# A two-layer block on one core: the experts' tail and the second projection as one program, worked token tile by token tile

## The reference

```
y = y + combine[:, e:e + 1] * (h @ w_down[e])      # 32 experts, 2 of them per token
h = h + y
x = rmsnorm(h, final_norm_g)                       # result of the first block
h = rms_norm(x, norm_gain)                         # start of the second block
proj = h @ w_in                                    # 1024 x 8448
qa, ka, va, qb, kb, vb, ga, gb, mg = split(proj)
```

## Time and profile before

| | us |
|---|---|
| median of three runs (range) | 1345.03 (1338.94 to 1348.52) |
| profiled execution: time / span of its instructions | 1341.23 / 1339.5 |
| loop of experts, first to last product | 485.1 to 708.3 |
| rows of experts loaded back, sums and norms on DVE | 716.7 to 740.2 |
| PE without an instruction | 719.4 to 741.9 |
| first product of the second projection | 747.8 |
| its units 0, 1, 2 end | 766.9, 778.4, 789.9 |

### The profile page before, as it was taken

How to read it: one execution, slowest core, us unless ns; L and a number is a source line. 1 busy time by engine, 2 the same in 40 slices (tenths; PEclk the granted TensorE clock), 3 DMA queues, 4 the chain that set the end, 5 groups by cost and what they waited for, 6 DMA issues and landing times. The chain is left out here.

```text
span 1339.5 us, 24510 instructions
## 1 busy us (share of the span) xinstructions
PE 1233.6 (92%) x10443; PEld 967.9 (72%) x10443; DVE 549.3 (41%) x973; ACT 491.6 (37%) x859; POOL 153.8 (11%) x210
## 2 busy tenths in 40 slices
PE   5999999999979769999881899999999999999988
PEld 5787775699959545655540798888896678888888
DVE  3433563344364223333225423344437764553242
ACT  4324537603244401111112424455547654332230
POOL 4000003200000001111100001122210015300000
PEclk9999999999999969999996899999999999999999
DMA  4332100000029699999995445422217118222031
GB/s 158 115 104 72 32 1 0 10 4 4 4 70 390 231 367 418 419 418 420 417 409 198 119 139 132 104 92 71 91 32 95 65 36 282 63 64 94 1 110 48
DMA packets 92664, 197.63 MB, mean 148 GB/s; under 512 B 9687, under 2 KB 73261, under 8 KB 79629
## 3 DMA queue, kind: packets, MB, share of 16 engines
q1 hardware_dynamic: 87228, 185.57, 39.6%
q0 software_dynamic: 4752, 8.40, 1.7%
q10 hardware_dynamic: 576, 2.10, 0.4%
HBM read 186.05 MB, written 17.86 MB: 152 GB/s over the span
## 5 line engine op out<-in xcount | busy, mean ns | idle before, releaser
L650 DVE TENSOR_TENSOR w_in_low<-w_in_raw,w_in_high 128x2048 fp32r<-128x2048 f32 x20 | 45.9, 2293 | 116.4 <-ACT w_in_high L642 116.4
L1935 PE MATMUL hidden_ps<-w_gate,gathered_t 128*64 128x256 f32 x384 | 92.2, 395 | 0.3 <-DVE gathered_t L2030 0.3
L1935 PE MATMUL hidden_ps<-w_up,gathered_t 128*64 128x256 f32 x384 | 92.2, 395 | 0.0
L602 PE MATMUL proj_ps<-block_in_high,w_in_low 128*128 128x512 f32 x232 | 90.5, 390 | 0.0
L602 PE MATMUL proj_ps<-block_in_low,w_in_high 128*128 128x512 f32 x232 | 90.5, 390 | 0.0
L602 PE MATMUL proj_ps<-block_in_high,w_in_high 128*128 128x512 f32 x232 | 90.4, 390 | 0.0
L1476 PE MATMUL wo_ps<-w_out_high,wo_x_high 128*128 128x256 f32 x256 | 74.2, 290 | 3.5 <-DVE w_out_low L661 3.5
L2775 PE MATMUL gate_ps<-block_in_high,gate_w_high 128*128 128x512 f32 x192 | 76.0, 396 | 1.0 <-PEq L2444 1.0
L2775 PE MATMUL gate_ps<-block_in_low,gate_w_high 128*128 128x512 f32 x192 | 74.9, 390 | 0.0
L2775 PE MATMUL gate_ps<-block_in_high,gate_w_low 128*128 128x512 f32 x192 | 74.8, 390 | 0.0
L1476 PE MATMUL wo_ps<-w_out_high,wo_x_low 128*128 128x256 f32 x256 | 73.2, 286 | 0.0
(11 more groups left out here) (474 smaller groups left out, 3072.5 us busy)
## 6 DMA issues: line engine op xcount, KB each, us to landing
w_down<-exp_w_down_dram SPq DMA_DIRECT2D x27, 1024.0 KB, 27.9
w_gate<-exp_w_gate_dram SPq DMA_DIRECT2D x24, 1024.0 KB, 20.2
w_up<-exp_w_up_dram SPq DMA_DIRECT2D x24, 1024.0 KB, 23.1
w_in_raw<-w_in_dram SPq DMA_DIRECT2D x20, 1024.0 KB, 5.6
slot_scratch_and_keys<-w_in_dram SPq DMA_DIRECT2D x14, 1024.0 KB, 5.4
vb<-w_in_dram SPq DMA_DIRECT2D x6, 1024.0 KB, 5.8
gate_w_raw_odd<-w_in_dram SPq DMA_DIRECT2D x6, 1024.0 KB, 6.1
slot_scratch_and_keys<-exp_w_down_dram SPq DMA_DIRECT2D x5, 1024.0 KB, 30.2
```

Of the source, the lines that this page charges most:

```text
L602: m = pe.matmul(out, a(k)[i], b(k)[j], start=(k == 0 and i + j == 0), stop=(k == n - 1 and i == 1))
L650: dve.tensor_tensor(self.part[1][n % 2], self.slot(n), self.part[0][n % 2], ALU.subtract).then_inc(self.low, 1)
L1935: x = pe.matmul(g_bank[e % 2][a * CAP:(a + 1) * CAP, 0:DE], xT[e % 2][:, k, :], w[:, k, :], start=(k == 0), stop=(k == KC - 1))
```

## The change

- Experts' tail and second projection become one program (`SecondProjection`), without the barrier and the clearing of semaphores between them. The barrier behind the projection stays.
- The four token tiles go through one after the other: sum of rows, squares (ACT), weighted squares by one reduction on DVE (`weigh`, instead of the multiplied `h` and a second pass of squares on ACT), token factors, diagonal, turning, high and low halves in 8 pieces of 128 x 128 per tile, then the products of units 0 and 1 for this tile. `h` is multiplied by the final gain after the last tile. The gain of both norms is one product of columns, for which one more row of parameters is loaded at the start of the kernel (SP's queue, eighteenth small load).
- The weights of units 0 and 1 are loaded before the rows come back and split early; unit 2 gets parts of its own (`keep_third`), so it doesn't wait for the jobs of unit 0.
- The pick of the bias rows goes behind unit 0 of the last tile, and `add_windows` behind the low half of unit 2 and the four gain products on DVE.
- In the experts' loop the next list is formed in expert 19 and 20 (`LIST_AT`), into a second buffer that a copy takes over at the round's start; POOL's gather for it moves ahead of the last three writes. The choice weights are worked out after the loop.

```diff
+LIST_AT = 20
...
+    def keep_third(self, n, parts):
+
+        self.third = n
+        for part, room in zip(self.part, parts):
+            part.append(room)
+
...
-        if n >= 2:
+        if n >= 2 and n != self.third:
...
+    def take(self, dve, rnd):
+        dve.wait_ge(self.ready, rnd + 1)
+        dve.tensor_copy(self.idx[:, :, :], self.coming[:, :, :]).then_inc(self.taken, 1)
...
-                        if i < NP:
+                        if i == 1:
+                            pool.wait_ge(lists.taken, rnd + 1)
+                            pool.sem_inc(seen)
+                        if i <= NP:
                             if i >= GB:
                                 pool.wait_ge(turned, rnd * NE + 2 * (i - GB) + 2)
                                 pool.sem_inc(seen)
-                            lists.gather(pool, i)
+                            if i < NP:
+                                lists.gather(pool, i, idx)
+                            else:
+                                pool.wait_ge(lists.ready, rnd + 2)
+                                pool.sem_inc(seen)
+                                lists.gather(pool, 0, lists.coming)
...
+                        if e == LIST_AT:
+                            lists.product(pe, rnd + 1, at[:, :, :], h_bank[(e + 1) % 2])
...
+                        if e == LIST_AT - 1:
+                            lists.mark(dve, rnd + 1, at[:, :, :])
...
+        sp.dma_start(wts.slot(0), w[:, :, cols[0]:cols[0] + UNIT]).then_inc(const["second_w_in"], 16)
+        sp.dma_start(self.fin_g[:, :], self.A["final_norm_g"].rearrange("(a d) -> a d", a=1).broadcast_to([P, D])).then_inc(self.gain_in, 16)
+        wts.load(sp, 1)
+        sp.wait_ge(*rows_written)
+        for c in range(TT):
+            sp.dma_start(self.yg[c], self.rows[c]).then_inc(self.got[c], 16)
+        self.bias.load(sp)
+        v_rows = T["v_dram"].rearrange("(c p) w -> p c w", p=P)
+        early = 2 * HW // UNIT
+        for u in range(2, len(wts.cols)):
+            wts.load(sp, u)
+            if u == 2:
+                self.bias.store(sp)
...
+    def turn(self, pe, c):
+        pe.wait_ge(self.diag_ready, c + 1)
+        for j in range(self.NTURN):
+            if c:
+                pe.wait_ge(self.low_st, KC * (c - 1) + KC - self.NTURN + j + 1)
+            for k in range(j, KC, self.NTURN):
+                m = pe.matmul(self.turn_at(k), self.h[:, c, k * P:(k + 1) * P], self.diag[:, c, :], start=True, stop=True)
+            m.then_inc(self.turned, 1)
+
...
+        self.turn(pe, 0)
+        for c in range(TT):
+            for u in range(self.EARLY):
+                if c == 0:
+                    wts.wait(pe, u)
+                at = slice(c % 2 * UNIT, (c % 2 + 1) * UNIT)
                 for k in range(KC):
...
+                    pe.wait_ge(self.low_st, KC * c + k + 1)
+                    for a, b in ((0, 0), (0, 1), (1, 0)):
+                        m = pe.matmul(bank[c // 2 * self.EARLY + u][:, at], hT[a][:, k, c * P:(c + 1) * P], wts.parts(u, k, slice(0, UNIT))[b],
                                       start=(k == 0 and a + b == 0), stop=(k == KC - 1 and a == 1))
...
+                    if c + 1 < TT and u == self.EARLY - 1 and k == KC - 3:
+                        self.turn(pe, c + 1)
+                if c % 2:
+                    m.then_inc(self.ready, 1)
+                if c == TT - 1 and u == 0:
+                    self.bias.pick(pe)
...
+        def highs(c):
+            act.wait_ge(self.fin, 3 * c + 2)
+            act.activation(self.ws[:, c:c + 1], self.ws[:, c:c + 1], ACT.Sqrt).then_inc(self.root, 1)
+            act.wait_ge(self.fin, 3 * c + 3)
+            act.activation(const["fin_rstd"][:, c:c + 1], self.inv[:, c:c + 1], ACT.Sqrt).then_inc(self.root, 1)
+            if c == 0:
+                act.wait_ge(self.gains_made, 1)
+            for k in range(KC):
+                if k < self.NTURN:
+                    act.wait_ge(self.turned, self.NTURN * c + k + 1)
+                else:
+                    act.wait_ge(self.low_st, KC * c + k - self.NTURN + 1)
+                act.activation(self.hT[0][:, k, c * P:(c + 1) * P], self.turn_at(k), ACT.Copy, scale=self.fin_cols[:, k:k + 1]).then_inc(self.high_st, 1)
+
+        square(0)
+        for c in range(TT):
+            if c + 1 < TT:
+                square(c + 1)
+            highs(c)
+        act.preload_act_table_set("natural_log_exp_and_others")
+        wts.split_high(act, self.EARLY)
...
+            if u >= self.EARLY and self.last_job.get(u - 1) == n - 1:
+                wts.split_high(act, u + 1)
...
+        def weigh(c):
+            dve.wait_ge(self.squared, c + 1)
+            dve.tensor_tensor_reduce(out=self.h_sq[c % 2], in0=self.h_sq[c % 2], in1=self.gain_sq, scale=1.0 / D, scalar=0.0, op0=ALU.mult, op1=ALU.add,
+                                     accum_out=self.ws[:, c:c + 1]).then_inc(self.weighed, 1)
+
+        def scale(c):
+            ss, ws, inv = (x[:, c:c + 1] for x in (self.ss, self.ws, self.inv))
+            dve.tensor_scalar(ss, ss, 1.0 / D, EPS, ALU.mult, ALU.add).then_inc(self.fin, 1)
+            dve.wait_ge(self.weighed, c + 1)
+            dve.wait_ge(self.fin, 3 * c + 1)
+            dve.scalar_tensor_tensor(out=ws, in0=ss, scalar=EPS, in1=ws, op0=ALU.mult, op1=ALU.add).then_inc(self.fin, 1)
+            dve.reciprocal(inv, ss).then_inc(self.fin, 1)
+            dve.wait_ge(self.root, 2 * c + 1)
+            dve.reciprocal(const["second_scale"][:, c:c + 1], ws).then_inc(self.gains_made, 1)
+            dve.wait_ge(self.gains_made, c + 2)
+            dve.tensor_scalar(self.diag[:, c, :], const["ident"][:, :], const["second_scale"][:, c:c + 1], None, ALU.mult).then_inc(self.diag_ready, 1)
+
+        def low(c):
+            for k in range(KC):
+                dve.wait_ge(self.high_st, KC * c + k + 1)
+                dve.scalar_tensor_tensor(out=self.hT[1][:, k, c * P:(c + 1) * P], in0=self.turn_at(k), scalar=self.fin_cols[:, k:k + 1],
+                                         in1=self.hT[0][:, k, c * P:(c + 1) * P], op0=ALU.mult, op1=ALU.subtract).then_inc(self.low_st, 1)
...
+        for c in range(2):
+            for j in range(2):
+                add(c, j)
+        weigh(0)
+        for c in range(TT):
+            scale(c)
+            if c + 2 < TT:
+                add(c + 2, 0)
+            elif c + 1 < TT:
+                weigh(c + 1)
+            low(c)
+            if c + 2 < TT:
+                add(c + 2, 1)
+                weigh(c + 1)
+        wts.split_low(dve, self.EARLY)
+        for c in range(TT):
+            dve.tensor_tensor(self.h[:, c, :], self.h[:, c, :], self.fin_g[:, :], ALU.mult).then_inc(self.gained, 1)
+        self.bias.add_windows(dve)
+        dve.wait_ge(self.bias.stored, 64)
+        for m, (u, *_) in enumerate(jobs):
+            if u >= self.EARLY and self.last_job.get(u - 1) == m - 1:
+                wts.split_low(dve, u + 1)
```

More of the change, by code:

```diff
@@ L1780, in first_gather @@
         pool.wait_ge(self.ready, 1)
-        self.gather(pool, 0)
+        self.gather(pool, 0, self.coming)
 def load_matrix(sp, A, M, name, j, e):
@@ L1877, in _ @@
                                 load_matrix(sp, A, M, "down", j, j)
[L1878 to L1882, removed]
+                second.sync(sp, (places_free, last + 1))
             @block.gpsimd
@@ L1910, in _ @@
                     pool.sem_inc(places_free)
-                    pool.wait_ge(lists.ready, rnd + 2)
-                    pool.sem_inc(seen)
-                    lists.gather(pool, 0)
                 pool.wait_ge(x_in[0], last * (16 * len(range(0, NP, GB))) + 16)
+                second.gpsimd(pool)
             @block.tensor
@@ new lines, in tensor, with head_sums @@
+    def tensor(self, pe):
+        jobs, normed, plain, bank, hT, wts, const, T = self.jobs, self.normed, self.plain, self.bank, self.hT, self.wts, self.const, self.T
+        def head_sums(i):
+            pe.wait_ge(self.sq_low, i + 1)
+            if i == 0:
+                pe.wait_ge(self.bias.added, 2)
+            if i >= 2:
+                pe.wait_ge(self.logged, i - 1)
+            for j in range(2):
+                m = pe.matmul(self.sums[i % 2][:, :], const["heads_exact"][:, :], self.sq_part[j][:, i % (2 - j), :], start=(j == 0), stop=(j == 1))
+            m.then_inc(self.summed, 1)
+        self.turn(pe, 0)
[4 more added lines that the diff above has]
+                at = slice(c % 2 * UNIT, (c % 2 + 1) * UNIT)
@@ new lines, in tensor, with tokens, some @@
+                    if c + 1 < TT and u == self.EARLY - 1 and k == KC - 3:
[4 more added lines that the diff above has]
+                    self.bias.pick(pe)
+        for n, (u, kind, x, dst, gain, perm) in enumerate(jobs):
+            if u < self.EARLY:
+                continue
+            wts.wait(pe, u)
+            if n >= self.NBANK:
+                o = n - self.NBANK
+                if o in normed:
+                    pe.wait_ge(self.qk_st, normed.index(o) + 1)
```

(23 more changed lines are left out.)

516 lines of the change are left out of this document (223 added, 293 removed).

## The result

The changed kernel takes 1355.87 us (median of five runs, 1351.7 to 1356.73) against 1343.24 (five runs of the kernel before): a ratio of 1.0087, 95% interval 1.0062 to 1.0111. It is slower by about 12 us. The profiled executions say 1351.7 against 1341.23, spans 1350.0 against 1339.5, so 10.5 us to explain.

What follows compares the result with a forecast made beforehand. Weights set the experts' pace; for the change, what counted was when PE can start unit 3. To 1341.23 profiled, 6.8 for that start and 0.3 for the parameter row gave 1348.3, or 1352 on the median; range 1341 to 1360.

Steps and rivals of the forecast that it cites:

- Windows ready (T): On DVE, behind unit 2's low half and four gain products: bias-row windows ready at 767.7, 15 us later than before.
- The 128-column low half: On DVE, eight per token tile: 0.34 us each on a line through two sizes, 0.32 in a row, 2.6 for eight.
- Rival B: ACT and DVE alternate on 128-column pieces: 5.6 us a tile, not 2.6; +19, 1364; chance 0.16 with other late pieces.
- From T to unit 3's parts: Store, then unit 3's load landing at T + 22.7 = 790.4, high half 1.9, low half 2.29: ready at 794.6.
- Units 0 and 1: In the projection PE follows each tile and ends units 0 and 1 near 761, against 778.4: 17.5 us ahead.
- The clock: PE's granted clock is 0.50 after the hole: 2.1 us charged, so unit 3 starts in effect at 796.7.
- Parameter row: One more small load adds an issue of 0.3 to 0.6 us in front of PE's first work; 0.3 taken.
- Rival A: Early start kept if the store doesn't hold unit 3's weights: -2.2 to 0, or all 17.5 won; chance 0.12.

Runs made afterwards that it cites:

- Experiments 1: Changed kernel with unit 3's load ahead of the bias-row store on SP, DVE's wait kept: 1349.63 us, ratio 1.0029 to the kernel before.
- experiments 2: Changed kernel with DVE's wait for the store moved behind unit 4's first job, SP's order kept: 1352.62 us, ratio 1.0073 to the kernel before.
- experiment 3: Changed kernel with unit 3's load ahead of the store on SP and DVE's wait moved back: 1344.62 us, ratio 0.9993 to the kernel before.
- 6: Changed kernel with DVE adding the windows ahead of the four gain products: 1352.43 us, ratio 1.0035 to the kernel before.
- Experiment 7: Changed kernel with the store behind unit 4's load on SP and DVE's wait behind unit 4's first job: 1332.63 us, ratio 0.9882 to the kernel before.
- experiment 5: Kernel before with the bias rows stored from 16 partitions in two transfers, nothing else: 1343.86 us, ratio 0.9978 to the kernel before.
- experiment 4: Changed kernel with the bias rows stored in two transfers from 16 partitions, not four from 8: 1347.45 us, ratio 1.0018 to the kernel before.

## Why the prediction was right, step by step

The mechanism was the forecast one, at each link: an early start, units 0 to 2 done ahead of time, the windows late behind DVE's list, store and load behind them, a hole of PE of some 20 us ended by unit 3's low half, and a cold clock behind it. 1355.87 lies in the range, near the upper end of the forecast's own (1349 to 1356). Experiments 1 to 3 show the hole to be two queues', 6 that it follows the windows, 7 that it was the whole loss. The sum was too small: +7 forecast (+4 to +11 with its bounds), +10.5 in the profiles and +8 to +15 by the ratio, with 11.7 in the middle. Its terms:

- **Windows ready (T)**: 767.7 forecast, 771.6 measured. This is the term that was mis-sized, by 3.9. The tiles began at 725.09 and not 722.4: 0.8 because the stage as a whole stands later, the rest mostly (a wait of 1.65 on DVE) because I let unit 1's weights be there when DVE came. They were asked for at 711.10 and reached ACT only at 720.9, 9.8 later, among unit 0, the gain and the last written rows. The four tiles took 35.3 and not 33.6; DVE waits 3.73 for the last turn (the row at 757.69 above), which stands behind six pieces of unit 1 of tile 2 (`k == KC - 3` comes after the sixth; the prediction counted five).
- **The 128-column low half**: taken at 0.34 alone and 0.32 in a row. It is 346 ns, and two in a row take 0.60. The rule of the Trainium skill, "VectorE: DVE Perf Modes", section "The TRN2 errata", was right that small pieces pay a fixed time; the estimate of 0.26 from its table was too low, and the line through the earlier trace rows was the better guide. (With 0.26 the sum would have been nearer 2 us lower, 32 pieces at 0.06, than the 1 it says.) Rival B is out: eight pieces take 2.7 us in tiles 1 to 3, where B had 5.6, and 3.8 in the first tile, whose first four come at 0.8 each because ACT waits for PE's turns there (the granted clock is 0.50 from 730 to 735).
- **From T to unit 3's parts**: 26.9 forecast, 27.1 measured (771.56 to 798.69). The lags were carried over from the kernel before, where the load stood behind the store too but, as experiment 5 shows, was held by its slot; that they agreed is partly luck.
- **Units 0 and 1**: their end was put near 761, as if PE only followed the tiles, and an end after 766 was to be the sign of B. It came at 767.1, but not by the pieces. PE's own work was not added up: two units (23 us), three turns of 1.7 to 1.8 and the pick of 1.9 make 30 of the 31.2 us from its first product at 735.91, with a single wait of 0.24 among them (at 741.46). The late end cost nothing by itself, since unit 2's end at 778 is still 20.8 ahead of unit 3's start; what PE's pace cost is the late last turn, under T.
- **The clock**: 2.1 charged; unit 3 takes 14.2 (798.75 to 812.93) where 11.5 is a unit, so 2.7.
- **Parameter row**: 0.3 charged, PE's first work starts at 13.34 and not 13.29. Nothing.
- **Rival A** named the right condition, a store that doesn't hold unit 3's weights, and doubted it rightly as long as nothing else is moved. Its price of 17.5 was too high: units 0 and 1 end at 767.1, 11 ahead and not 17.5, since PE itself sets that end. Experiment 7 gets 12.0.

## What to carry to other kernels

When a change lets an engine start earlier, list what else hangs on the side paths that now come later: a transfer that waits for a small result holds everything behind it on its queue (48 us without an issue here), and what it held up before may have been nothing. Before costing the transfer's duration, ask what stands behind it and whether the order can be changed; here moving it past two loads, together with one wait, was worth 2%, a store of twice the speed 0.7%. A removed hole moves to the next thing behind the same item (experiment 3), so move the item past all loads that come due while it runs.

## What was not expected of the hardware

- The load behind the store lands when the store does, whichever way the store is cut. In the changed kernel and experiments 2, 4, 6 and 7, where a load follows the store directly, it lands 3.8 to 4.0 us after the store's last transfer, although in experiment 4 it is asked for 8.7 us sooner behind the store than in the others. So there it takes 15.5 us from its request to ACT's high half (776.93 to 792.43), and 12.7 in the changed kernel (781.67 to 794.37).
- The store's issues on SP's queue take 10.05 us for four transfers from 8 partitions and 1.35 for two from 16, for the same bytes. The partitions alone don't explain it: of the four, the first two take 0.86 and 0.69 and the other two 4.13 and 4.23, and in experiment 4 it is the load behind the two that takes 4.22. In both the queue is held from the third issue on; by what, no run here shows.

```profile
L2112 SPq DMA_DIRECT2D bias_rows_dram<-qk_a x4: 693/2494/4232, 771.6 to 777.4; - x4
L2111 SPq DMA_DIRECT2D bias_rows_dram<-qk_a x2: 603/653/703, 775.5 to 776.3; - x2
```

The numbers behind the colons are the shortest, median and longest issue in ns, of the changed kernel and of experiment 4.
